# Expert weights on two issuing queues: ten units in flight, the second layer's loads issued by ScalarE

## What is computed

```python
def clamped_swiglu(h):
    glu, lin = jnp.split(h, 2, axis=-1)
    glu = jnp.minimum(glu, SWIGLU_LIMIT)
    lin = jnp.clip(lin, -SWIGLU_LIMIT, SWIGLU_LIMIT)
    return glu * jax.nn.sigmoid(SWIGLU_ALPHA * glu) * (lin + 1.0)
...
    h = layer_norm(DEEPNORM_ALPHA * x + mix, ln1_w, ln1_b)
    ffn = moe_ffn(h, router_w, router_b, moe_w1, moe_b1, moe_w2, moe_b2)
    return layer_norm(DEEPNORM_ALPHA * h + ffn, ln2_w, ln2_b)
...
    def expert_block(args):
        xb, e = args
        return clamped_swiglu(xb @ w1[e] + b1[e]) @ w2[e] + b2[e]
```

## Time and profile before

| | us |
|---|---|
| median of 3 runs | 1396.55 (1396.24 to 1399.17) |
| profiled execution, with what lies around its span | 1397.37 |
| its span | 1395.6 |
| TensorE busy | 1280.6 (92%) |
| VectorE busy | 455.0 |
| ScalarE busy | 177.1 |
| first expert's first product starts | 454.73 |
| last expert's second layer ends | 1381.6 |

### The profile page before, as it was taken

One profiled execution on the slowest core, in us unless ns is written; L12 is line 12 of the kernel. 1 busy time (PEld: TensorE's weight loads), 2 busy tenths in 40 slices (PEclk: granted clock), 3 DMA queues, 4 the chain that ended last, 5 costly groups with the idle time before them and its releaser, 6 DMA issues.

```text
span 1395.6 us, 15452 instructions
## 1 busy us (share of the span) xinstructions
PE 1280.6 (92%) x6184; PEld 663.2 (48%) x6184; DVE 455.0 (33%) x919; ACT 177.1 (13%) x304; POOL 5.0 (0%) x22
## 2 busy tenths in 40 slices
PE   8999999967998999998999999999899999899996
PEld 6877877866865344332333333333233332333332
DVE  3769856243635412212212121221212212132123
ACT  1342214121101101000100001101010100000101
POOL 1000000000000000000000000000000000000000
PEclk9999999998997999999999999999999999999998
DMA  9734344312565899999999999999999999999990
GB/s 292 219 108 138 106 136 151 121 61 91 196 249 233 331 428 428 429 428 428 429 428 429 429 428 429 428 429 428 428 428 428 428 429 429 429 429 429 428 386 31
DMA packets 76629, 458.23 MB, mean 328 GB/s; under 512 B 11299, under 2 KB 44438, under 8 KB 52022
## 3 DMA queue, kind: packets, MB, share of 16 engines
q1 hardware_dynamic: 67888, 453.00, 79.7%
q10 hardware_dynamic: 8710, 4.80, 1.3%
HBM read 456.73 MB, written 1.05 MB: 328 GB/s over the span
## 4 chain that ended last, share of the span: by engine, by line
DMA 46%; PE 21%; DVE 1%; issue 1%; SPq 0%; ACT 0%; DVEq 0%
DMA ring<-in_moe_w 46%; PE banks L1019 14%; PE banks L1042 3%; PE banks L989 1%; PE banks L1071 1%; PE banks L966 0%; PE banks L1059 0%; PE banks L1027 0%; PE banks L1079 0%; DVE arena L1693 0%; SPq L333 0%; DVE small L1689 0%; DVE arena L1696 0%; DVE arena L1614 0%; ACT arena L648 0%
## 5 line engine op out<-in xcount | busy, mean ns | idle before, releaser
L1019 PE MATMUL banks<-ring,arena 128*64 128x512 f32 x1536 | 363.1, 625 | 60.7 <-DMA ring<-in_moe_w 60.6
L1019 PEld LDWEIGHTS banks<-ring,arena 128*64 128x64 f32 x1536 | 112.9, 144 | 303.9 <-issue 219.4
L724 PE MATMUL banks<-acc_xT,ring 128*128 128x256 f32 x928 | 209.3, 385 | 0.8 <-DVE acc_xT L1148 0.8
L724 PEld LDWEIGHTS banks<-acc_xT,ring 128*128 128x128 f32 x928 | 176.9, 193 | 31.3 <-issue 6.3
L1610 DVE TENSOR_SCALAR arena<-banks 128x512 f32<-128x512 f32 x32 | 22.1, 692 | 489.3 <-PE banks L1019 489.3
L1042 PE MATMUL banks<-ring,arena 128*64 128x512 f32 x512 | 117.1, 599 | 0.0
L1042 PE MATMUL banks<-yT,arena 128*64 128x512 f32 x512 | 115.3, 592 | 0.0
L1622 DVE COPY arena<-banks 64x512 f32<-64x512 f32 x32 | 22.2, 694 | 241.3 <-PE banks L1042 241.3
L656 ACT ACTIVATE arena<-arena 128x512 f32<-128x512 f32 x32 | 20.1, 630 | 531.9 <-DVE arena L1610 531.9
L1042 PEld LDWEIGHTS banks<-ring,arena 128*64 128x64 f32 x512 | 34.0, 137 | 81.6 <-issue 57.3
L1042 PEld LDWEIGHTS banks<-yT,arena 128*64 128x64 f32 x512 | 36.8, 137 | 73.1 <-issue 73.1
(11 more groups left out here) (356 smaller groups left out, 929.3 us busy)
## 6 DMA issues: line engine op xcount, KB each, us to landing
ring<-in_moe_w SPq DMA_DIRECT2D x128, 2048.0 KB, 23.9
yT<-in_moe_w SPq DMA_DIRECT2D x32, 2048.0 KB, 21.6
arena<-in_moe_w SPq DMA_DIRECT2D x16, 2048.0 KB, 22.6
acc_xT<-in_moe_w SPq DMA_DIRECT2D x16, 2048.0 KB, 27.6
ring<-in_w_in SPq DMA_DIRECT2D x31, 1024.0 KB, 5.6
ring<-in_w_branch SPq DMA_DIRECT2D x8, 1024.0 KB, 5.0
ring<-in_w_out SPq DMA_DIRECT2D x4, 1024.0 KB, 4.9
acc_xT<-in_x SPq DMA_DIRECT2D x1, 1024.0 KB, 5.0
```

What stands on the lines that cost most here:

```text
L724: last = mm(b[:, j * SEQ:(j + 1) * SEQ], w[:, k, j * P:j * P + P], xT[:, k, :], start=k == 0, stop=k == KD - 1)
L1019: last = mm(bank[i][64 * ct:64 * ct + 64, :], xg[:, 2 * c + k, col:col + CAP], w[:, k, i * FF + ct * 512:i * FF + ct * 512 + 512], start=F ...
```

## The change

- `NFIRST = NW1`: all four units of the first layer have a place for even and one for odd experts, ten places with the two of the second layer. The new place is a second unit in `arena`, which grows by 1472 columns; `yT` changes from a second-layer place to a first-layer place.
- SP issues ten units before the experts begin. In the loop it issues only first-layer units, of expert n + 2 as expert n uses its own. The second-layer units are issued by ScalarE, on its own queue, behind its copy of the second layer's result.
- The broadcasts of `ln2_w` and `ln2_b` go. Four rows of 2 KB are loaded to `wa` instead, and products with a row of ones (`widen`) spread them into PSUM: the scale in the last expert's second layer, copied by ScalarE to `arena`; the shift behind the last combine, read from PSUM.
- `weights` and `add_sum` of the last pair move from behind the last first layer to between its third and fourth unit.

```diff
-NFIRST = 3
+NFIRST = NW1
...
-        even_unit = [arena_unit, unit_of(0), unit_of(1)]
-        odd_unit = [unit_of(2), unit_of(3), acc_xT.rearrange("p a b -> p (a b)")]
-        each_unit = [unit_of(4), unit_of(5), yT[:, :, :, :].rearrange("p a b c -> p (a b c)")]
+        even_unit = [arena_unit[0], arena_unit[1], unit_of(0), unit_of(1)]
+        odd_unit = [yT[:, :, :, :].rearrange("p a b c -> p (a b c)"), unit_of(2), unit_of(3), acc_xT.rearrange("p a b -> p (a b)")]
+        each_unit = [unit_of(4), unit_of(5)]
...
+            sp.wait_ge(S["yA_ready"], 2)
+            load(0, 0, 1)
             sp.wait_ge(S["chunk_used"], used_up("wb", 1, 1))
-            load(0, 0, 1)
+            load(0, 0, 2)
             sp.wait_ge(S["chunk_used"], used_up("wb", 0, 1))
-            load(0, 0, 2)
+            load(0, 0, 3)
             sp.wait_ge(S["acc_ready"], 4)
-            load(0, 0, 3)
             load(0, 0, 4)
             load(0, 0, 5)
+            load(1, 1, 0)
             sp.wait_ge(S["chunk_used"], used_up("wo", 1))
-            load(1, 1, 0)
+            load(1, 1, 1)
             sp.wait_ge(S["chunk_used"], used_up("wo", 3))
-            load(1, 1, 1)
             load(1, 1, 2)
+            load(1, 1, 3)
 
             with sp.Fori(0, NPAIR - 1) as p:
                 for odd in range(2):
                     n = p * 2 + odd
-                    for c in range(NFIRST):
+                    for c in range(NW1):
                         sp.wait_ge(S["expert_chunk_used"], n * NU + c + 1)
                         load(n + 2, odd, c)
-                    for c in range(NFIRST, NU):
-                        sp.wait_ge(S["expert_chunk_used"], n * NU + c + 1)
-                        load(n + 1, 1 - odd, c)
...
-            act.dma_start(ln2_w[:, :], A["ln2_w"].to_broadcast([P, D])).then_inc(S["ln2_in"], 16)
-            act.dma_start(ln2_b[:, :], A["ln2_b"].to_broadcast([P, D])).then_inc(S["ln2_in"], 16)
...
+            for j in range(4):
+                act.dma_start(ln2_rows[32 * j:32 * j + 1, :], A["ln2_w" if j < 2 else "ln2_b"][:, 512 * (j % 2):512 * (j % 2) + 512]).then_inc(S["ln2_in"], 16)
...
                 act.wait_ge(S["expert_chunk_used"], n * NU + NU)
                 nc.scalar.activation(y_pair[64 * u:64 * u + 64, 0:512], bank[4][0:64, :], ACT.Copy).then_inc(S["ypair_act"], 1)
+                if load_next:
+                    for c in range(NW1, NU):
+                        act.dma_start(expert_unit(c), expert_source(n + 1, c)).then_inc(landed_of(c), 16)
...
+            act.wait_ge(S["ln2_w_wide"], 1)
+            nc.scalar.activation(ln2_w, banks[:, 0:2, :].rearrange("p a b -> p (a b)"), ACT.Copy).then_inc(S["ln2_w_ready"], 1)
...
                 for c in range(NW1):
+                    if last_pair and c == NW1 - 1:
+                        weights(NPAIR - 1)
+                        pe.wait_ge(S["wselT_ready"], NPAIR)
+                        add_sum()
...
                 if last_pair:
-                    pe.wait_ge(S["comb_used"], NPAIR * 4)
-                    pe.wait_ge(S["wselT_ready"], NPAIR)
-                    add_sum()
+                    pe.wait_ge(S["ln2_in"], 64)
+                    widen(0)
+                    widen(1).then_inc(S["ln2_w_wide"], 1)
...
+            def widen(j):
+
+                return mm(bank[(0, 1, 4, 5)[j]][:, :], ones[32 * j:32 * j + 1, :], ln2_rows[32 * j:32 * j + 1, :], start=True, stop=True, tile_position=(32 * j, 0))
...
             combine(NPAIR - 1, NE, P, on_sum=True)
+            widen(2)
+            widen(3).then_inc(S["ln2_b_wide"], 1)
...
-            dve.wait_ge(S["ln2_in"], 32)
+            dve.wait_ge(S["ln2_w_ready"], 1)
...
+                dve.wait_ge(S["ln2_b_wide"], 1)
                 dve.wait_ge(S["rs_ready"], 6 + half)
```

More of the change, by code:

```diff
@@ L125, in encoder_layer @@
         yT = sb("yT", [P, NBR, HEADS, SEQ])
-        ARENA = 18432
+        ARENA = 19904
         arena = sb("arena", [P, ARENA])
@@ L211, in encoder_layer @@
         m = At(0)
[L212 removed]
+        arena_unit = [m(UNIT), m(UNIT)]
         h_tok = m(2, D)
         y_acc = m(2, D)
[L215 removed]
         b1_all = m(512)
@@ L220, in encoder_layer @@
         g1, g2, g3 = m(512), m(512), m(512)
+        ln_w, ln_b = at(m.o, D), at(m.o + D, D)
+        ln2_w = at(m.o - D, D)
         actT = m(4, P)
@@ L223, in encoder_layer @@
         wselT = m(2, P)
+        wsel = m(2, P)
         sel = m(2, 2 * CAP)
-        wsel = m(2, P)
         esel = m(CAP)
@@ L652, in weights, with expert @@
                 nc.scalar.activation(wselT.rearrange("p a b -> p (a b)"), bank[7][:, 0:256], ACT.Copy).then_inc(S["wselT_ready"], 1)
-            def expert(n, u, weights_of=None, gather_next=None):
+            def expert(n, u, weights_of=None, gather_next=None, load_next=False):
                 act.wait_ge(S["gmin_ready"], n + 1)
@@ L664, in expert @@
                 nc.scalar.activation(y_pair[64 * u:64 * u + 64, 0:512], bank[4][0:64, :], ACT.Copy).then_inc(S["ypair_act"], 1)
+                if load_next:
+                    for c in range(NW1, NU):
+                        act.dma_start(expert_unit(c), expert_source(n + 1, c)).then_inc(landed_of(c), 16)
             gathered(0)
-            expert(0, 0)
-            with act.Fori(0, NPAIR - 1) as p:
-                expert(p * 2 + 1, 1, p, p + 1)
-                expert(p * 2 + 2, 0)
-            expert(NE - 1, 1, NPAIR - 1)
+            expert(0, 0, load_next=True)
+            with act.Fori(0, NPAIR - 2) as p:
+                expert(p * 2 + 1, 1, p, p + 1, load_next=True)
+                expert(p * 2 + 2, 0, load_next=True)
+            expert(NE - 3, 1, NPAIR - 2, NPAIR - 1, load_next=True)
+            expert(NE - 2, 0)
+            weights(NPAIR - 1)
+            expert(NE - 1, 1)
             act.wait_ge(S["items_ready"], 1)
@@ L1092, in _ @@
                 second_layer(p * 2 + 2, 0, p * 2 + 3)
-            first_layer(NE - 1, 1, NPAIR - 1)
-            weights(NPAIR - 1)
+            first_layer(NE - 1, 1, NPAIR - 1, last_pair=True)
             second_layer(NE - 1, 1, last_pair=True)
             combine(NPAIR - 1, NE, P, on_sum=True)
+            widen(2)
+            widen(3).then_inc(S["ln2_b_wide"], 1)
             pe.wait_ge(S["items_ready"], 1)
@@ L1109, in _ @@
                 pe.wait_ge(S["comb_used"], n_items * 4 + (NPAIR + 1) * 4)
+                for j in range(4):
+                    ins = widen(j)
+                    if j == 1:
+                        ins.then_inc(S["ln2_w_wide"], 1)
                 add_sum(alone=True)
@@ L1692, in _ @@
                 V.reciprocal(small[:, 314:315], small[:, 314:315]).then_inc(S["rs_req"], 1)
-                link(V.scalar_tensor_tensor(y, total, small[:, 312:313], ln2_w[:, :].rearrange("p (a b) -> p a b", a=2), ALU.subtract, ALU.mult))
+                link(V.scalar_tensor_tensor(y, total, small[:, 312:313], ln2_w.rearrange("p (a b) -> p a b", a=2), ALU.subtract, ALU.mult))
+                dve.wait_ge(S["ln2_b_wide"], 1)
                 dve.wait_ge(S["rs_ready"], 6 + half)
                 if half == 0:
-                    V.scalar_tensor_tensor(y_acc[:, 0, :], y_acc[:, 0, :], small[:, 314:315], ln2_b[:, :], ALU.mult, ALU.add).then_inc(S["out_ready"], 1)
+                    V.scalar_tensor_tensor(y_acc[:, 0, :], y_acc[:, 0, :], small[:, 314:315], banks[:, 4:6, :].rearrange("p a b -> p (a b)"), ALU.mult, ALU.add).then_inc(S["out_ready"], 1)
                     dve.wait_ge(S["out_ready"], 1)
@@ L1700, in _ @@
                         piece = slice(512 * dh, 512 * dh + 512)
-                        V.scalar_tensor_tensor(y_acc[:, 1, piece], y_acc[:, 1, piece], small[:, 314:315], ln2_b[:, piece], ALU.mult, ALU.add)\
+                        V.scalar_tensor_tensor(y_acc[:, 1, piece], y_acc[:, 1, piece], small[:, 314:315], bank[4 + dh][:, :], ALU.mult, ALU.add)\
                             .then_inc(S["out_ready"], 1)
```

8 lines of the change are left out of this document (4 added, 4 removed).

## The result

| | before | after |
|---|---|---|
| median | 1395.44 us (16 runs) | 1387.99 us (16 runs, 1386.61 to 1395.20) |
| ratio | | 0.9950, 95% interval 0.9938 to 0.9961 |
| span of the profiled execution | 1395.6 | 1385.7 |
| last byte of the weight stream | 1358.8 | 1355.3 |
| expert 30 ends | 1350.56 | 1338.05 |

The changed kernel is faster by 0.5%, where the prediction said slower by 0.3%. The first rival had 1388.0. Single executions of one kernel lie some microseconds apart (1386.6 to 1395.2 here), and a trace shows one of them, so a microsecond or two between the traces of two kernels can be chance.

A forecast was written before the change was run, and what follows sets the result against it. The prediction took a stream of 2 MB units, then a dependent tail, as the bound. Expert 30's end +1.9, the tail +2.0 and norm +0.2 gave +4.1 us on 1396.55: 1400.7, range 1385 to 1404 including rival 1.

The forecast's parts named there:

- Rival 1: Weight stream: both queues share at once, second-layer units overtake first-layer ones; −8.5 us, 1388.0 us; chance 0.25.
- What bounds the kernel: Expert stage: a stream of 2 MB units at 428 GB/s sets the time until near the end, then dependent work.
- The units' prices: Expert stage: 4.90 us to transfer one unit, 29.4 us for an expert's six, 25.9 us of TensorE per expert.
- Tenth unit and hole: Start of expert stage: one more unit loaded early gains 4.9 us, a dry stretch near 480 costs 3.9 net; −1.0 us.
- The split queues: Steady expert stage: ScalarE's units served in order of issue behind two to three of SP's; no change per expert.
- The end: Last two experts: expert 30 ends 1.9 us later, at 1352.5; the tail to expert 31's second layer takes 33.0, +2.0 us.
- Norm: After the last combine: ScalarE's copy of the scale is hidden, spreading the shift delays its first use; +0.2 us.
- the prediction's signs: Trace: in order, ScalarE's units take 23 us or more, waits in second layer; shared, about 20, waits in first layer.
- Rival 2: Weight stream: nothing but the tenth unit counts; −1 to −3 us, or added waits cancel it, 1395.5; chance 0.12.
- rival 3: Weight stream: two streams in HBM change the transfer rate, 2.7 us either way; chance 0.05.
- The chances: Whole kernel: 0.58 for the in-order forecast; with rivals together faster 0.32, same 0.21, slower 0.47.

The follow-up runs named there:

- unit 4 early: Against the changed kernel: ScalarE issues the next expert's unit 4 once TensorE has used this one's, ahead of its copy; 1386.10 us, ratio 0.9922 to the kernel before.
- one-queue run: Against the changed kernel: SP issues all weight loads, ten places kept, in the order in which places come free; 1397.88 us, ratio 1.0016 to the kernel before.

## Why the prediction was wrong

- **What bounds the kernel** was read rightly: a full stream at 428 GB/s, then dependent work. The units' prices (4.90, 29.4, 25.9 us) held: 428 GB/s as before, and 25.8 us for expert 30 in the run with unit 4 early, where it waits for nothing (1311.49 to 1337.33).
- **Tenth unit and hole**: −1.0 forecast, −3.5 measured by the last byte. The hole was 4.4 us of the 5 forecast, counted by bytes as the forecast counts the 1.1 us before; and the hole that the kernel before had from 1345 to 1350 us, 308 GB/s or 1.4 us, went too, which the sum had left out. It mattered little: by the one-queue and the unit-4 runs the last byte doesn't set the end.
- **The split queues: the step that failed.** From 788 packets ahead of SP's first one I took a standing line of some 50 descriptors in order of issue. It was a delay at the start. In the kernel after, ScalarE's load waited 3.5 us, in which some 100 of SP's packets (1.5 MB) passed, and then the queues shared; 50 descriptors of 16 KB for each engine would have been 13 MB. SP had about five units ahead, not two to three, and they did not hold ScalarE's back. The text named this case itself ("wrong if the line of 50 descriptors is counted in bytes"), and the earlier trace rows held the hint: the load in question landed 4.2 us later than its neighbour, no more, whatever the number of descriptors. The rule of the Trainium skill ("DMA: Bandwidth & Descriptors", Queues, rings and completion order), round-robin between queues by packet, agrees with every stretch measured here but for those first 3 to 4 us (counted in the profile's packets, one row each for 16 KB rows; whether the Trainium skill means the same by a packet isn't shown); the first rival, with its 1388.0, rests on such sharing.
- **The end**: expert 30 was forecast to end at 1352.5 and ended at 1338.05; rival 1 had 1339.9. That is the whole error of direction. The tail was forecast at 33.0 us and took 33.4: sum 3.70 (3.63 forecast), spreading 2.01 (2.04), second layer 8.50 at a granted clock of 0.50 in its first part (forecast in all 1.2 us more, measured 1.5). The moved sum is a cost, 2.3 to 2.7 us by two runs. The last two units were issued by SP, at 1334.00 and 1338.10; they landed by 1357.10, before the second layer began at 1362.92, and had no part in it.
- **Norm**: +0.2 forecast; from the end of the second layer to the first use of the shift 5.8 us, 5.6 before. ScalarE's copy of the scale took 1.02 us and was hidden.
- **Rival 1** named the mechanism, but that its total fits to 0.01 us (1388.0 against 1387.99) is luck: it counts from a median of three runs, 1396.55, where sixteen give 1395.44, and its −8.5 us stands against −7.5 by the medians and −9.9 by the spans. Its detail was off: it had TensorE wait in the first layer only; the waits for a DMA are 26.8 us on L1055 and 16.4 + 10.4 on L1032. So two of the prediction's signs don't separate the cases: the waits lie on both lines, and ScalarE's second unit takes 23.3 us to landing, the first 14.0 ("23 us or more" was to mean in order). The end of expert 30, and no hole near 1350 us, do. **Rival 2** (only the tenth unit) falls by the one-queue run, **rival 3** by 428 GB/s with one stream and with two.
- **The chances**: 0.58 rested on one event of one size against one counter-example in the same trace. Two rows that speak against each other called for the reading under which both hold (a start delay, then sharing).

What the parts of the change were worth, then: all of it but the second queue +0.16% or 2.2 us (the moved sum with the spreading 2.3 to 2.7, the tenth place 2.0 off that by the trace of the one-queue run, about 0.5 by its median; no run has the tenth place, or the new norm rows, by itself); the second queue, by the order in which it lets the units land, 9 to 10 us.

## What to carry to other kernels

When one stream of loads bounds the work, ask for each load in the queue whether something behind it is needed sooner: refilling places as they come free puts the next stage's data ahead of this one's, and issuing in order of need won as much from one queue as a second queue did. Total bytes and the last byte then matter less than how much dependent work is left when the last waited-for unit lands. Work that is moved off the tail belongs under a stall of the engine that does it, where it also keeps the engine's clock up, not ahead of a unit that has landed or is about to.

## What the runs showed of the hardware

Two queues with work pending were served packet for packet (257 against 251; 236 against 237), so bytes went by the size of the rows, 3.34 against 0.97 MB for 16 KB against 4 KB. A load issued while the other queue had large loads in flight got its first packet 2.9 to 4.1 us after its issue (3.5 and 4.0 in the two kernels), against 1.0 to 1.9 otherwise; its cause wasn't found. A stream of 16 KB rows held 428 GB/s on one queue and on two.
